# Sixteen more up tiles in the wide form: its range begins at tile 48 where it began at tile 64

## The chip, the cores and the metric

The kernel runs on one NeuronCore of one Trainium2 chip. The metric is the time of one execution on the device in microseconds, measured on that core. The time of before is 1027.47 us, the median of three runs (1025.19, 1027.47, 1031.39).

## What is computed

One decoder layer for a prompt of 256 tokens and eight samples of four tokens: a joint projection, two attention mixers, an output projection with LayerNorm, and then the part in which the change lies, PEER. There each token's query picks, from 128 x 128 experts per head, 16 experts for each of 8 heads. The reference computes it as

```
a = gelu(einsum('cpkd,cd->cpk', u_tab[e], h))
out = einsum('cpk,cpkd->cd', g * a, v_tab[e])
```

with `u_tab` and `v_tab` of 16,384 rows by 1,024. For the 256 prompt tokens the kernel takes every expert instead of gathering: it multiplies h by the whole of u, 128 tiles of 128 experts ("up"), applies GELU, weighs the result by a gate that is zero where an expert was not picked, and multiplies by the whole of v, 128 tiles again ("down"). The 32 sample tokens gather their rows of u and v instead.

## The kernel before, in words

The numbers need nearly fp32 accuracy, so each product is made of three: operands are split into a high part rounded to the fast fp32 form and a low part (the rest), and hi*hi, hi*lo and lo*hi are added in PSUM.

**One up tile.** SP loads a tile of u (128 x 1024 floats, 512 KB) into one of four ring slots. ScalarE writes its high part `w_hi` with a copy (`high`, line 1198, the copy at 1204), VectorE its low part `w_lo` by a subtraction (`low`, line 1579, the instruction at 1583), TensorE multiplies eight blocks of 128 rows with h. `halves` gives the semaphore values at which the low part of a tile is there. The result of tile n lies in PSUM bank n % 4, first 256 columns. ScalarE applies GELU (line 1456) into `u_out`, which has two buffers, and SP stores it to DRAM (`store`, line 460; `activations`), from where the down tiles read it back. 32 results, those of positions 64 to 95, stay in SBUF (`keep`) and are not stored; tiles are numbered here by position in the order of work. Because ring slots, PSUM banks and `w_hi` are all four deep, the high part of tile n + 4 is made after tile n's product is done.

**Two forms of the product.** The narrow form (`project` with `parts`, lines 639 and 630) has for each block three products of 256 columns: w_hi with h_hi (L635), w_hi with h_lo (L636), w_lo with h_hi (L637). The wide form (`project_wide`, line 1085) has two: w_hi with h_lo and h_hi side by side, 512 columns in one product (L1091), and w_lo with h_hi, 256 columns (L1093), into the bank's second half. The two halves of the bank then have to be added: ScalarE copies the second half to SBUF (`u_half`, line 1451), VectorE adds it to the first (line 1595), and only then comes the GELU. There is one buffer `u_half`.

**Which tile has which form** is said by `WIDE` (line 54), a range of positions. TensorE runs narrow loops over tiles 4 to `WIDE.start`, a wide loop over the range, and narrow ones again (lines 1097 to 1102). VectorE's program is laid out by Python: `low_next` (line 1588) puts out the next low part, ahead of it the addition for the tile four earlier if that one is in `WIDE`, and behind it a row dot (`row_dot`, line 1606) of the samples if one is due. The candidate lists and the routing of the prompt tokens (`top16`, `route`) are interleaved with `low_next` by `pace`, which counts work and not time. So VectorE runs everything in one fixed order. ScalarE has `gelu` (line 1441) and `gelu_then_high` (line 1458): narrow tiles have GELU, then the cast of tile n + 4; wide ones have the wait for the store, the copy to `u_half`, the cast, the wait for the addition and the GELU. Before, `gelu` takes its form from the first tile of its loop.

**Order on the queues.** SP alternates (`experts_in`, line 464): for each r it waits till the low part of the tile four earlier is there, issues the load of tile n, then waits for the GELU of tile n - 6 and issues its store. Before tile n's result is touched, ScalarE waits till the store of tile n - 2 has landed (line 1449). GpSimd meanwhile issues small indirect DMAs (`gates_out`, line 570) and gathers of 512 KB (`row_of_u`, line 578), each gather behind a row dot. At the first kept tile ScalarE waits once for the ninth row dot (line 1484), because `keep` lies over the candidate lists.

Of the kernel before, what the change touches and what calls it, by code (L numbers as in the profile page):

```python
# [26 lines left out]
KEPT, KEPT_AT = 32, 64  # L27
# [23 lines left out]
NCAND = sum(ROWLEN)  # L51
PACE, PACE_Q, PACE_LISTS, PACE_ROUTE = 1.2, 2.0, 2 / 3, 0.5
LIST_DOTS = 8
WIDE = range(64, 104)
SLOPES = [2.0 ** (-(h + 1)) for h in range(8)]


# [77 lines left out]
def trunk(nc, xT, w_in, w_gate, w_out, w_q, keysT, uT, v, u_rows, w1, pe_cmp, w2, vecs, ln2_rows, cache_sb, cache_nsa,  # L135
# [3 lines left out]
    with ctx:  # L139
# [259 lines left out]
        def filled(n):  # L399

            return n % 4, 16 * (n // 4 + 1)
# [3 lines left out]
        U_ALONE = NE - GN // 8  # L405
# [6 lines left out]
        def place(n):  # L412

            if AT_OUT <= n < AT_Q:
                return OUT_PLACE[n - AT_OUT]
            return n % 4 if n < AT_U + U_ALONE else 4 + n % 2
# [206 lines left out]
        def _(pe):  # L623
# [28 lines left out]
            def halves(i, n):  # L652

                return part_lo[n % 4], 2 * i + (2 * (n // 4) + 1), 2 * i + (2 * (n // 4) + 2)
# [424 lines left out]
            def experts_up(first, last):  # L1079
                with pe.Fori(first, last) as i:  # L1080
                    for r in range(4):
                        pe.wait_ge(u_act, 4 * i + r + 1)
                        project((AT_U + r) % 4, h_parts, r, halves(i, AT_U + r), width=DT)

            def project_wide(slot, bank, lows):

                for kd in range(KD):
                    if kd % 4 == 0:
                        pe.wait_ge(lows[0], lows[1 + kd // 4])
                    block_ = slice(kd * 128, (kd + 1) * 128)  # L1090
                    mm(ps[:, bank, :].rearrange("p (a t) -> p a t", a=2), w_hi[slot][:, block_],  # L1091
                       h_both[:, :, kd * T:kd * T + DT], start=kd == 0, stop=False)
                    ins = mm(ps[:, bank, DT:2 * DT], w_lo[slot][:, block_], h_hi[:, kd, 0:DT], start=False, stop=kd == KD - 1)  # L1093
                    if kd % 4 == 3:
                        ins.then_inc(w_mm, 1)

            experts_up(1, WIDE.start // 4)
            with pe.Fori(WIDE.start // 4, WIDE.stop // 4) as i:
                for r in range(4):
                    pe.wait_ge(u_act, 4 * i + r + 1)  # L1100
                    project_wide((AT_U + r) % 4, r, halves(i, AT_U + r))
            experts_up(WIDE.stop // 4, U_ALONE // 4 - 1)

# [84 lines left out]
        def _(act):  # L1188
# [9 lines left out]
            def high(ring_slot, arrived, slot, half=None, used=None):  # L1198

                act.wait_ge(full[ring_slot], arrived)  # L1200
                if used is not None:
                    act.wait_ge(w_mm, used)
                x = slice(0, D) if half is None else slice(half * D // 2, (half + 1) * D // 2)
                nc.scalar.copy(w_hi[slot][:, x], ring[:, ring_slot, x]).then_inc(part_hi, 2 if half is None else 1)  # L1204
# [233 lines left out]
            act.sem_inc(u_act, 4)  # L1438
            act.sem_inc(g_sb, 4)

            def gelu(i, r, first=0):

                act.wait_ge(w_mm, 8 * i + 2 * (AT_U + first + r + 1))
                if first == KEPT_AT:
                    out = keep[:, bass.ds(4 * i + r, 1), :].rearrange("p a t -> p (a t)")
                else:
                    out, kept_before = u_out[:, r % 2, :], KEPT if first > KEPT_AT else 0
                    if first + r >= 2:
                        act.wait_ge(spill[r % 2], 32 * i + 16 * ((first + r - kept_before) // 2))
                if first >= WIDE.start and first < WIDE.stop:  # L1450
                    nc.scalar.copy(u_half[:, :], ps[:, r, DT:2 * DT]).then_inc(u_lo, 1)
                    n = AT_U + first + r + 4
                    slot, value = filled(n)
                    high(slot, 16 * i + value, place(n))
                    act.wait_ge(u_sum, 4 * i + (first - WIDE.start + r + 1))
                A(out, ps[:, r, 0:DT], ACT.Gelu_apprx_tanh).then_inc(u_act, 1)  # L1456

            def gelu_then_high(i, r, first=0):

                gelu(i, r, first)  # L1460
                n = AT_U + first + r + 4
                slot, value = filled(n)
                high(slot, 16 * i + value, place(n))
# [14 lines left out]
            A(pick[:, 0, 2, 64:128], pick[:, 0, 2, 64:128], ACT.Exp).then_inc(rt_exp, 1)  # L1478
            for r in range(4):
                gelu_then_high(3, r, 4)  # L1480
            with act.Fori(4, KEPT_AT // 4 - 1) as i:
                for r in range(4):
                    gelu_then_high(i, r, 4)
            act.wait_ge(u_dot, LIST_DOTS + 1)
            assert WIDE.start == KEPT_AT and WIDE.stop == U_ALONE - 8
            with act.Fori(0, KEPT // 4) as i:
                for r in range(4):
                    gelu(i, r, KEPT_AT)
            with act.Fori(0, (U_ALONE - 8 - KEPT_AT - KEPT) // 4) as i:
                for r in range(4):  # L1490
                    gelu(i, r, KEPT_AT + KEPT)

            act.wait_ge(rt_exp_in, 4)
            A(sgate[:, :], sgate[:, :], ACT.Exp).then_inc(rt_exp, 1)
# [862 lines left out]
```

## Time and profile before

| | |
|---|---|
| median of three runs | 1027.47 us (1025.19 to 1031.39) |
| the profiled execution: its time | 1030.56 us |
| the profiled execution: span from first to last instruction | 1028.8 us |
| TensorE busy | 1011.6 us, 98% |
| VectorE busy | 818.3 us, 80% |
| ScalarE busy | 546.0 us, 53% |
| GpSimd busy | 371.5 us, 36% |
| mean granted TensorE clock | 0.995 |

Durations below come from the one profiled execution, whose own time lies 3.1 us over the median. In the rows PE is TensorE, PEld its weight loads, DVE VectorE, ACT ScalarE, POOL GpSimd and SP SyncE; L1583 is line 1583 of the kernel. Matmuls overlap one another, so a product's spacing to the next, not its own duration, is what it costs. A row that ends in brackets names how long the engine was idle just ahead of the instruction and what ended that.

### The profile page before, as it was taken

The numbers are of one execution on the slowest core, as the hardware profiler recorded it, in microseconds if no ns is written. First come the engines' busy times: TensorE is split into PE (matmuls) and PEld (weight loads), VectorE is DVE, ScalarE is ACT, GpSimd is POOL, SyncE is SP. The second block draws the span as 40 slices with busy tenths as digits, with TensorE's granted clock in tenths as the row PEclk, the third lists the DMA queues.
The fourth block names the chain that finished last, engine by engine and source line by source line (L and its number), as shares of the span: only waits on it lengthen the run. The fifth ranks groups of instructions, "written<-read, shape, count | busy, mean of one in ns | idle before, by whom it ended". The sixth has DMA issues, their size and how long they took to land.

```text
span 1028.8 us, 21635 instructions
## 1 busy us (share of the span) xinstructions
PE 1011.6 (98%) x6669; PEld 898.4 (87%) x6669; DVE 818.3 (80%) x1819; ACT 546.0 (53%) x1036; POOL 371.5 (36%) x287
## 2 busy tenths in 40 slices
PE   8999999999999999999999999999999999999997
PEld 7997747999999999998888999988878888888876
DVE  5344277786889988879998699988878888999888
ACT  5435576454545444456555655555555555555553
POOL 0244400000067888888887875011110101111000
PEclk9999999999999999999999999999999999999999
DMA  8756889344588899999999966778888889888763
GB/s 273 258 219 219 304 271 314 122 154 134 189 216 229 216 295 292 332 325 283 279 279 273 259 130 178 254 238 310 323 298 307 282 296 308 305 301 308 254 223 126
DMA packets 123281, 261.77 MB, mean 254 GB/s; under 512 B 29104, under 2 KB 70080, under 8 KB 121408
## 3 DMA queue, kind: packets, MB, share of 16 engines
q1 hardware_dynamic: 89280, 198.31, 57.3%
q0 software_dynamic: 33664, 62.30, 22.1%
q10 hardware_dynamic: 288, 0.59, 0.2%
q8 instruction: 21, 0.34, 0.1%
q14 instruction: 28, 0.23, 0.1%
HBM read 236.83 MB, written 26.38 MB: 256 GB/s over the span
## 4 chain that ended last, share of the span: by engine, by line
PE 59%; DMA 2%; DVE 1%; issue 1%; DVEq 0%; ACT 0%; SPq 0%; ACTq 0%
PE ps L1147 10%; PE ps L1149 10%; PE ps L1148 10%; PE ps L1091 7%; PE ps L636 5%; PE ps L635 5%; PE ps L637 5%; PE ps L1093 4%; PE ps L1124 3%; DMA a_in<-activations 1%; DMA ring<-in_v_dram 1%; DVE w_lo L1583 1%; PE ps L1138 0%; PE ps L1169 0%; DVE y_lo L2124 0%
## 5 line engine op out<-in xcount | busy, mean ns | idle before, releaser
L1583 DVE TENSOR_TENSOR w_lo<-ring,w_hi 128x512 fp32r<-128x512 f32 (+1 forms) x440 | 383.7, 879 | 109.2 <-ACT w_hi L1204 91.8
L1204 ACT CAST w_hi<-ring 128x512 fp32r<-128x512 f32 (+1 forms) x437 | 338.0, 774 | 79.1 <-PE ps L1149 54.1
L574 POOL DMA_INDIRECT gates<-spread_out,spread_at x128 | 241.7, 1888 | 131.4 <-DVE spread_out L2039 82.4
L635 PE MATMUL ps<-h_both,w_hi 128*128 128x256 f32 (+1 forms) x808 | 234.4, 290 | 2.0 <-DVE w_lo L1583 1.8
L636 PE MATMUL ps<-h_both,w_hi 128*128 128x256 f32 (+1 forms) x808 | 230.1, 285 | 0.0
L637 PE MATMUL ps<-h_both,w_lo 128*128 128x256 f32 (+1 forms) x808 | 228.9, 283 | 0.0
L1147 PE MATMUL ps<-w_hi,y_hi 128*128 128x512 f32 x496 | 193.4, 390 | 1.5 <-DVE y_lo L2124 1.3
L1148 PE MATMUL ps<-w_hi,y_lo 128*128 128x512 f32 x496 | 193.0, 389 | 0.0
L1149 PE MATMUL ps<-w_lo,y_hi 128*128 128x512 f32 x496 | 193.0, 389 | 0.0
L635 PEld LDWEIGHTS ps<-h_both,w_hi 128*128 128x128 f32 x808 | 153.6, 190 | 3.5 <-DVE w_lo L1583 2.2
L636 PEld LDWEIGHTS ps<-h_both,w_hi 128*128 128x128 f32 x808 | 153.2, 190 | 0.0
L637 PEld LDWEIGHTS ps<-h_both,w_lo 128*128 128x128 f32 x808 | 151.8, 188 | 0.0
L600 POOL DMA_INDIRECT vrow<-in_v_dram,expert x32 | 36.4, 1136 | 256.2 <-DVE sacc L2149 235.4
L1147 PEld LDWEIGHTS ps<-w_hi,y_hi 128*128 128x128 f32 x496 | 93.1, 188 | 22.3 <-DVE y_lo L2124 2.6
L1091 PE MATMUL ps<-h_both,w_hi 128*128 128x512 f32 x320 | 111.5, 392 | 0.0
L1149 PEld LDWEIGHTS ps<-w_lo,y_hi 128*128 128x128 f32 x496 | 93.1, 188 | 19.6
L1148 PEld LDWEIGHTS ps<-w_hi,y_lo 128*128 128x128 f32 x496 | 93.1, 188 | 19.2
L1456 ACT ACTIVATE u_out<-ps 128x256 f32<-128x256 f32 x96 | 37.0, 385 | 125.7 <-PE ps L637 77.9
L1093 PE MATMUL ps<-h_both,w_lo 128*128 128x256 f32 x320 | 89.9, 281 | 0.0
L1527 ACT CAST y_hi<-a_in 128x256 fp32r<-128x256 f32 x92 | 37.5, 408 | 66.5 <-PE ps L1149 66.3
L1091 PEld LDWEIGHTS ps<-h_both,w_hi 128*128 128x128 f32 x320 | 60.0, 188 | 13.4
L1093 PEld LDWEIGHTS ps<-h_both,w_lo 128*128 128x128 f32 x320 | 60.4, 189 | 0.0
(392 smaller groups left out, 1493.8 us busy)
## 6 DMA issues: line engine op xcount, KB each, us to landing
ring<-in_uT_dram SPq DMA_DIRECT2D x128, 512.0 KB, 4.3
ring<-in_v_dram SPq DMA_DIRECT2D x128, 512.0 KB, 4.3
activations<-u_out SPq DMA_DIRECT2D x96, 128.0 KB
a_in<-activations SPq DMA_DIRECT2D x96, 128.0 KB, 4.2
ring<-in_w_in_dram SPq DMA_DIRECT2D x21, 512.0 KB, 5.5
gates<-spread_out SPq DMA_DIRECT2D x8, 1024.0 KB, 9.1
ring<-in_w_q_dram SPq DMA_DIRECT2D x16, 512.0 KB, 3.9
gates<-gates POOLq DMA_DIRECT2D x8, 1024.0 KB, 7.6
```

What stands on the lines that cost most here:

```text
L574: nc.gpsimd.indirect_dma_start(g_dram, bass.IndirectOffsetOnAxis(ap=spread_at[:, m:m + 1], axis=0), spread_out[:, m:m + 1], None, compute_ ...
L635: mm(out, hi, hi_, start=start, stop=False)
L636: mm(out, hi, lo_, start=False, stop=False)
L637: return mm(out, lo, hi_, start=False, stop=stop)
L1091: mm(ps[:, bank, :].rearrange("p (a t) -> p a t", a=2), w_hi[slot][:, block_], h_both[:, :, kd * T:kd * T + DT], start=kd == 0, stop=False)
L1093: ins = mm(ps[:, bank, DT:2 * DT], w_lo[slot][:, block_], h_hi[:, kd, 0:DT], start=False, stop=kd == KD - 1)
L1147: mm(out, hi, w_hi[slot][:, x], start=False, stop=False, skip_group_check=True)
L1148: mm(out, lo, w_hi[slot][:, x], start=False, stop=False, skip_group_check=True)
L1149: return mm(out, hi, w_lo[slot][:, x], start=False, stop=stop, skip_group_check=True)
L1204: nc.scalar.copy(w_hi[slot][:, x], ring[:, ring_slot, x]).then_inc(part_hi, 2 if half is None else 1)
L1527: nc.scalar.copy(y_hi[:, r % 2, :], a).then_inc(y_h, 1)
L1583: V.tensor_tensor(w_lo[slot][:, x], ring[:, ring_slot, x], w_hi[slot][:, x].bitcast(F32), ALU.subtract).then_inc(part_lo[ring_slot], 2 if ...
```

## The change

The range of wide tiles begins at 48. ScalarE's loop over tiles 20 to 63 is cut in two, the second of them wide, and `gelu` is told its form by an argument. TensorE's loops and VectorE's additions follow from `WIDE`. Nothing else changes: loads, stores, the kept tiles, the lists and the dots stay in their order.

```diff
@@ -51,7 +51,7 @@
-WIDE = range(64, 104)
+WIDE = range(48, 104)
@@ -1438,7 +1438,7 @@
-            def gelu(i, r, first=0):
+            def gelu(i, r, first=0, wide=False):
 
                 act.wait_ge(w_mm, 8 * i + 2 * (AT_U + first + r + 1))
                 if first == KEPT_AT:
@@ -1447,7 +1447,7 @@
                     out, kept_before = u_out[:, r % 2, :], KEPT if first > KEPT_AT else 0
                     if first + r >= 2:
                         act.wait_ge(spill[r % 2], 32 * i + 16 * ((first + r - kept_before) // 2))
-                if first >= WIDE.start and first < WIDE.stop:
+                if wide:
                     nc.scalar.copy(u_half[:, :], ps[:, r, DT:2 * DT]).then_inc(u_lo, 1)
                     n = AT_U + first + r + 4
                     slot, value = filled(n)
@@ -1478,17 +1478,20 @@
-            with act.Fori(4, KEPT_AT // 4 - 1) as i:
+            with act.Fori(4, WIDE.start // 4 - 1) as i:
                 for r in range(4):
                     gelu_then_high(i, r, 4)
+            with act.Fori(WIDE.start // 4 - 1, KEPT_AT // 4 - 1) as i:
+                for r in range(4):
+                    gelu(i, r, 4, True)
             act.wait_ge(u_dot, LIST_DOTS + 1)
-            assert WIDE.start == KEPT_AT and WIDE.stop == U_ALONE - 8
+            assert WIDE.start <= KEPT_AT and WIDE.stop == U_ALONE - 8
             with act.Fori(0, KEPT // 4) as i:
                 for r in range(4):
-                    gelu(i, r, KEPT_AT)
+                    gelu(i, r, KEPT_AT, True)
             with act.Fori(0, (U_ALONE - 8 - KEPT_AT - KEPT) // 4) as i:
                 for r in range(4):
-                    gelu(i, r, KEPT_AT + KEPT)
+                    gelu(i, r, KEPT_AT + KEPT, True)
```

## Rows read from the trace of the kernel before

**Rows 1.** The page, busy shares and the 40 slices.
```profile
PE 1011.6 (98%) x6669; PEld 898.4 (87%) x6669; DVE 818.3 (80%) x1819; ACT 546.0 (53%) x1036; POOL 371.5 (36%) x287
...
PEclk9999999999999999999999999999999999999999
```

**Rows 2.** TensorE's own waits from 372 us on: total us, times, longest us.
```profile
PE ps L635 <- DVE w_lo L1583: 1.4, 1, 1.4
PE ps L1147 <- DVE y_lo L2124: 1.3, 1, 1.3
```

**Rows 3.** First products of a block, narrow (372 to 457.4 us) and wide: min/median/max ns.
```profile
L635 PE MATMUL ps<-h_both,w_hi x240: 277/282/385, 371.8 to 457.1; 128*128 128x256 f32 x120
...
L1091 PE MATMUL ps<-h_both,w_hi x320: 389/393/394, 457.5 to 568.6; 128*128 128x512 f32 x160
```

**Rows 4.** A stretch: us, busy PE, PEld, DVE, ACT, POOL, clock, DMA, GB/s.
```profile
411.70:457.50 45.80, 45.80 (x387) 45.80 (x386) 37.43 (x104) 21.23 (x33) 38.19 (x24) 1.00 1.02 320
```

**Rows 5.** ScalarE's GELUs, 411.7 to 459 us, and their longest wait.
```profile
L1456 ACT ACTIVATE u_out<-ps x17: 384/385/389, 412.9 to 458.6; 128x256 f32<-128x256 f32 x17
...
  DMA activations<-u_out: 20.4, 13
```

**Rows 6.** Groups by line and shape, whole span: busy us, mean ns, idle before.
```profile
L1595 DVE TENSOR_TENSOR ps<-ps,u_half 128x256 f32<-128x256 f32 x40 | 17.1, 428 | 2.2 <-ACT u_half L1451 1.9
...
L1451 ACT COPY u_half<-ps 128x256 f32<-128x256 f32 x40 | 14.9, 373 | 13.8 <-PE ps L1093 8.8 <-DMA activations<-u_out 4.9
```

**Rows 7.** VectorE's groups, 411.7 to 457.5 us, the first.
```profile
L1583 DVE TENSOR_TENSOR w_lo<-ring,w_hi 128x1024 fp32r<-128x1024 f32 x18 | 21.7, 1224 | 8.4 <-ACT w_hi L1204 8.0
```

**Rows 8.** Timeline of ScalarE, wide tiles with a store: start us, us, instruction.
```profile
549.74 0.37 ACT L1451 COPY u_half<-ps 128x256 f32<-128x256 f32 x1
...
553.00 0.38 ACT L1456 ACTIVATE u_out<-ps 128x256 f32<-128x256 f32 x1
...
557.68 0.37 ACT L1451 COPY u_half<-ps 128x256 f32<-128x256 f32 x1 [1.60 <-DMA activations<-u_out]
...
558.90 0.39 ACT L1456 ACTIVATE u_out<-ps 128x256 f32<-128x256 f32 x1
...
570.36 0.37 ACT L1451 COPY u_half<-ps 128x256 f32<-128x256 f32 x1 [1.31 <-DMA activations<-u_out]
```

**Rows 9.** Timeline of VectorE: the ninth row dot; the low part of tile 63.
```profile
423.25 1.23 DVE L1609 CUSTOM_DVE_ANT_0 urow<-urow,hrow 128x1024 f32<-128x1024 f32 x1
...
450.67 1.23 DVE L1583 TENSOR_TENSOR w_lo<-ring,w_hi 128x1024 fp32r<-128x1024 f32 x1 [0.45 <-ACT w_hi L1204]
```

**Rows 10.** Timeline of ScalarE at tile 64.
```profile
460.49 0.38 ACT L1451 COPY u_half<-ps 128x256 f32<-128x256 f32 x1 [0.58 <-PE ps L1093]
460.75 1.06 ACT L1204 CAST w_hi<-ring 128x1024 fp32r<-128x1024 f32 x1
```

**Rows 11.** Timeline of SP: four stores of u_out.
```profile
406.90 0.35 SPq L462 DMA_DIRECT2D activations<-u_out  x1
...
453.04 0.34 SPq L462 DMA_DIRECT2D activations<-u_out  x1
...
553.40 0.34 SPq L462 DMA_DIRECT2D activations<-u_out  x1
...
567.28 0.35 SPq L462 DMA_DIRECT2D activations<-u_out  x1
```

**Rows 12.** DMA in 411.7 to 457.5 us, then in 546 to 572 us: median us to landing.
```profile
ring<-in_uT_dram SPq DMA_DIRECT2D x17, 512.0 KB, 6.2
...
DMA packets 3841, 7.06 MB, mean 271 GB/s; under 512 B 1462, under 2 KB 2339, under 8 KB 3841
...
ring<-in_uT_dram SPq DMA_DIRECT2D x9, 512.0 KB, 4.8
```

**Rows 13.** Timeline of ScalarE: the first and last of the 13 waited GELUs.
```profile
412.90 0.39 ACT L1456 ACTIVATE u_out<-ps 128x256 f32<-128x256 f32 x1 [1.11 <-DMA activations<-u_out]
...
458.58 0.39 ACT L1456 ACTIVATE u_out<-ps 128x256 f32<-128x256 f32 x1 [2.13 <-DMA activations<-u_out]
```

## The prediction, made before the changed kernel ran

> **What bounds the kernel now.** I read the page's busy shares and slices first: TensorE is busy for 98% of the span and its granted clock is full in every slice [rows 1]; the list of TensorE's own waits then has, after 372 us, just two of 1.4 and 1.3 us [rows 2]. So TensorE's instruction stream sets the time, and everything else counts only when it makes TensorE wait. The change touches sixteen up tiles, 48 to 63. By the forms of their products they lie ahead of the first wide product at 457.5 us [rows 3]. A narrow tile is 24 products (8 blocks by 3). The 240 first products between 371.8 and 457.1 us give 85.3 / 239 = 0.357 us a block, 2.855 us a tile; the 320 wide ones between 457.5 and 568.6 us give 111.1 / 319 = 0.348 us a block, 2.786 us a tile [rows 3]. Tile 48 then starts at 457.5 - 16 x 2.855 = 411.8 us. From there to 457.5 us VectorE works 37.4 of 45.8 us, and the DMA engines are full: share 1.02, 320 GB/s [rows 4]. The last thing to see there is that ScalarE, ahead of its GELUs, waits 20.4 us in 13 of 17 cases for an earlier store of u_out to land [rows 5]. That wait costs nothing today, because the ring runs four tiles ahead; it is what the change leans on.
>
> **The change, part by part.** *TensorE.* Each of the sixteen tiles loses 8 products of 256 columns with their weight loads, and 8 others grow from 256 to 512 columns. By the tile times above it saves 2.855 - 2.786 = 0.069 us a tile, **1.1 us** in all, the only gain. The sum of columns is unchanged, so there is no second source. The wide block's 0.348 us stands on 320 of them [rows 3]. TensorE: Matmul & The Clock Gate in the Trainium skill, section Back-to-back issue gap, gives about 131 ns for a 512-column product in a sustained stream, and N/2.4 + 2.5 ns for an isolated one; by the first a wide tile could not last over 2.1 us and the change would give some 12 us, by the second it would give 0.3 us. The rows contradict the first and lie near the second.
>
> *VectorE.* Sixteen additions of 428 ns [rows 6] are 6.8 us more. Its low parts of this stretch come with 8.4 us of idle time, 8.0 of it behind ScalarE's casts [rows 7]; 45.8 - 37.4 = 8.4 again. It fits, with 1.5 us left (the stretch itself shrinks by 1.1), so I cost it at nothing on the path; without that cover it costs up to 6.8 us less the room worked out below. The row dots and candidate lists stay where they are in VectorE's program; behind each addition wait that tile's GELU and the low part of the tile four later.
>
> *ScalarE.* Sixteen copies of 373 ns [rows 6] are 6.0 us. It is busy 21.2 of 45.8 us [rows 4], so the copies themselves are covered. What matters is the order. In the narrow form the GELU comes first, then the cast; in the wide form copy, cast, wait for the addition, GELU. In a tile that finds everything ready the copy starts at 557.68 and the GELU at 558.90, 1.22 us later [rows 8]; where VectorE or the ring is late it is more: the first of the eight wide tiles with a store has 549.74 and 553.00, 3.26 us [rows 8]; over these eight the delay averages 1.8 us. For tiles 48 to 63, with lists on VectorE, I take 1.8 too (bounds 1.2 and 3.3). ScalarE's one-time wait for the ninth row dot at tile 64 is covered: that dot starts at 423.25 us [rows 9], and tile 64 comes to ScalarE at 460.49 us [rows 10].
>
> *SP and the stores.* u_out has two buffers, so work on tile n's result may begin when the store of n - 2 has landed. The store is issued 0.4 us behind its GELU where SP is free (553.00 [rows 8], 553.40 [rows 11]); I take 0.5, since a load's issue often lies between. In the narrow form a round for two tiles is 0.5 plus the landing; in the wide form it is 1.8 + 0.5 plus the landing, against the 5.57 us that TensorE takes for two wide tiles. So a landing up to 5.2 us is free now, and only up to 3.3 us afterwards. SP also issues the loads of the ring in the same queue, one between two stores, so a late GELU holds back the next load as well; loads land in 6.2 us (median) in this stretch and 4.8 us in 546 to 572 us [rows 12]. Their chain (GELU, store and load issue 1.1, landing 6.2, cast and GELU 1.2) is 8.5 us for three tiles, 2.8 a tile, as long as TensorE's and no longer.
>
> What the landing will be is the unknown. **Upper bound:** in the 13 waited cases of rows 5 it ran from store to GELU at first 6.0 us (406.90 to 412.90), at last 5.5 (453.04 to 458.58) [rows 11, 13], and 5.2 in the mean. **Lower bound:** in the five waited cases of the wide tiles with a store it was at first 4.3 (553.40 to 557.68), at last 3.1 (567.28 to 570.36) [rows 8, 11], and 3.55 in the mean, with the DMA engines at 271 GB/s [rows 12]. These eight tiles went without a stall of TensorE [rows 2]. I take 4.2 us, between them and nearer to the second: a chain that has become slower also asks for fewer transfers, which shortens the queue it waits in. The Trainium skill points the same way (DMA: Bandwidth & Descriptors, Latency and other measured facts: HBM access 0.2 us on average and 2 us at high load); the two stretches agree in sign, and no run so far shows the 0.2 us.
>
> *Room.* TensorE needs the low part of tile n + 4 three tiles after it ends tile n, 8.36 us. From the copy it takes 0.27 to the cast, 1.06 for the cast, 0.1 and 1.22 for the low part [rows 9, 10], 2.7 us. So ScalarE may fall 5.6 us behind while VectorE is free; in the busiest place today only 2.7 is left (low part of tile 63 from 450.67 to 451.90, its tile from 454.65) [rows 9].
>
> *Sum.* Landing 4.2: 6.5 us for two tiles, 3.25 a tile, 0.46 over TensorE's; sixteen tiles fall 7.4 us behind, 5.6 are room, TensorE stalls 1.8 us. Behind tile 63 there are no stores for 32 tiles and the delay drains. 1.8 - 1.1 = **+0.7 us**. The profiled execution took 1030.56 us (span 1028.8), 3.1 us over the median of the three runs, so 1031.3 for it and 1028.2 for the median.
>
> **Rivals.** *The room holds everything.* With the landing at 3.55 a round is 5.85 us, sixteen tiles fall 2.2 us behind and TensorE never waits: -1.1 us, 1026.4. For it speak the eight wide tiles with stores; against it that they had fewer row gathers beside them and no lists.
>
> *The stores' round trip becomes the bound.* With the landing at 5.2 a round is 7.5 us, 3.75 a tile, and sixteen tiles fall 15.4 us behind; less 5.6 of room and 1.1 of gain that is +8.7 us, with the smallest room of 2.7 it is +11.6: 1036 to 1039. It is slower than before from a landing of 4.1 us, and by over 0.5% (5.1 us, about what a measurement of this kernel can tell from no change) from 4.8 us. For it: 5.2 us is what these very tiles show, and DMA is full in them. Against: stores and loads come more slowly once it binds.
>
> *VectorE takes over.* If its waits of 8.0 us behind the casts stay as they are, the additions make it 6.8 us late; with room 2.7 to 5.6 TensorE stalls 1.2 to 4.1 us, net 0 to +3: 1027.5 to 1030.5. This lies in the forecast's own range.
>
> *The wide product costs less here than among the kept tiles.* To bring 5.1 us, a wide tile would have to fall to 2.855 - 5.1 / 16 = 2.54 us, 0.317 a block, where the quickest and slowest of its products differ by 5 ns in all 320 [rows 3]: 0.01, and about 1022 us. (The 131 ns of the page named above would be such a case.)
>
> *The change does not do what it says.* The form is chosen in three places: TensorE's loop, the test on VectorE and ScalarE's flag. All three follow, so this has 0.02; the time would be 1027.5.
>
> **How the numbers follow.** Forecast (stalls of 0.5 to 5 us, VectorE's case in it) 0.53; room holds 0.22; round trip 0.20; no effect 0.02; cheaper wide product 0.01; something unseen 0.02, taken as faster. Slower by over 0.5% is the round trip's 0.20 and 0.02 from the forecast's tail: 0.22. Faster by over 0.5% is 0.03, as 1.1 us is the whole gain. Within 0.5% is the rest, 0.75. The three runs of before spread from 1025.19 to 1031.39, so the lower end is -1.1 and 2.3 for that spread, 1024; the upper end takes in the middle of the round trip's case, 1036.
>
> **What would show it.** Right: the first product of the wide form comes near 411.8 us; tiles of 2.79 us up to about the tenth; ScalarE's waits for stores well over 20 us and now ahead of the copies; one or a few stalls of TensorE behind low parts, 1 to 5 us in all, between 435 and 475 us; landings near 4.2 us. Wrong: no stall at all (room holds), stalls over 6 us with landings of 5 and more (round trip), or VectorE without idle time there while the copies wait for nothing (VectorE's case). A gain over 5 us, or stalls far behind 500 us, would mean a mechanism that I have not seen.

## The result and the profile after

| | before | after |
|---|---|---|
| median (range) of 20 runs each, us | 1027.7 (1024.94 to 1031.97) | 1033.48 (1028.65 to 1040.73) |
| ratio | | 1.0048, interval 1.0033 to 1.0063 |
| profiled execution, us (span) | 1030.56 (1028.8) | 1030.98 (1029.3) |

The change makes the kernel 4.9 us slower (1027.7 x 0.0048; 3.4 to 6.5 by the interval). The two profiled executions differ by 0.4 us only, and that must not be read as the effect. The one of before lay about 3 us above its median and the one of after 2.5 us below: before had a wait of TensorE at 372 us [rows 2], another at 364 us, and a low clock about 160 us, all ahead of tile 48 and absent there in after. So I compare a stretch: the tiles 48 to 103, by their first products. The forms table of after gives its wide ones; the second line is the narrow form.

```profile
L1091 PE MATMUL ps<-h_both,w_hi x448: 388/393/632, 406.3 to 569.8; 128*128 128x512 f32 x150
L635 PE MATMUL ps<-h_both,w_hi x568: 277/282/384, 270.4 to 666.7; 128*128 128x256 f32 x190
```

There are 448 wide products for 320: 56 tiles. They take 569.8 - 406.3 = 163.5 us. Before, the same tiles took 568.6 - 411.8 = 156.8 us [rows 3]. The median of a product is as before; the maximum of 632 ns is new. The busy shares and the chain that ended last, from the page, and TensorE's waits from 400 to 575 us:

```profile
PE 1011.0 (98%) x6541; PEld 890.6 (87%) x6541; DVE 824.6 (80%) x1835; ACT 549.5 (53%) x1052; POOL 362.0 (35%) x287
```
```profile
PE 84%; DVE 8%; DMA 3%; ACT 2%; issue 2%; ACTq 0%; DVEq 0%; SPq 0%
PE ps L1147 11%; PE ps L635 11%; PE ps L1149 11%; PE ps L1148 11%; PE ps L636 11%; PE ps L637 11%; PE ps L1091 4%; PE ps L1124 3%; DVE w_lo L1586 3%; PE ps L1093 2%; DMA activations<-u_out 2%; PE ps L723 2%; ACT w_hi L1204 1%; DVE urow L1612 1%; PE ps L1018 1%
```
```profile
PE ps L1091 <- DVE w_lo L1586: 4.8, 5, 2.1
```

TensorE is still 98% busy, so the first line tells nothing. The chain does: stores of u_out have 2% of it and low parts 3%; in the chain of before, which could be followed back over only 63% of the span, u_out does not stand. And TensorE now waits for low parts ahead of wide products. Measured from block to block, the lost time is 2.29 us (at 447.61), 1.69 (462.11), 0.38 (465.38), 0.73 (477.32), 0.20 (527.75) and 0.48 (545.02): 5.8 us. The view of waits has less because it counts only from the end of the product ahead. The block behind each of these six is 0.07 to 0.11 us longer than the others, 0.5 us in all. 5.8 and 0.5 less the gain of 1.1 is +5.2 us, near the runs' +4.9, but it is one execution.

The largest of them can be followed back through four engines. POOL, SP, ScalarE, VectorE, TensorE in the timeline of after (start, duration, instruction, and in brackets the idle time ahead with its releaser):

```profile
437.09 0.99 POOL L581 DMA_INDIRECT urow<-in_u_rows_dram,expert  x1 [3.75 <-DVE sact L1612]
```
```profile
437.77 0.35 SPq L462 DMA_DIRECT2D activations<-u_out  x1
438.31 0.34 SPq L468 DMA_DIRECT2D ring<-in_uT_dram  x1
439.47 0.35 SPq L462 DMA_DIRECT2D activations<-u_out  x1
440.04 0.50 SPq L431 DMA_DIRECT2D ring<-in_uT_dram  x1
```
```profile
444.91 0.37 ACT L1451 COPY u_half<-ps 128x256 f32<-128x256 f32 x1 [5.61 <-DMA activations<-u_out]
445.18 1.05 ACT L1204 CAST w_hi<-ring 128x1024 fp32r<-128x1024 f32 x1
```
```profile
445.31 0.43 DVE L1598 TENSOR_TENSOR ps<-ps,u_half 128x256 f32<-128x256 f32 x1 [3.78 <-ACT u_half L1451]
446.33 1.23 DVE L1586 TENSOR_TENSOR w_lo<-ring,w_hi 128x1024 fp32r<-128x1024 f32 x1 [0.58 <-ACT w_hi L1204]
```
```profile
447.61 0.50 PE L1091 MATMUL ps<-h_both,w_hi 128*128 128x512 f32 x1 [2.13 <-DVE w_lo L1586]
```

One gather, two stores and two loads are issued within 3 us. The store of 437.77 lands at 444.91, 7.1 us later, and ScalarE stands for 5.6 of them **ahead of its copy**. Behind the copy stand the cast, VectorE's addition (VectorE is empty for 3.78 us) and the low part, and TensorE starts 2.7 us after the copy does, the distance that the prediction gave to this chain. Before, the same kind of wait stood ahead of GELUs [rows 5]. The next cast stood behind it there too; what is new is that copy, cast and addition stand between the wait and the next store.

The sum of ScalarE's waits for the stores did not grow, it moved ahead of the copies: from 400 to 575 us before had 25.1 us ahead of GELUs and 4.9 ahead of copies. ScalarE in after:

```profile
ACT u_half L1451 <- DMA activations<-u_out: 20.1, 13, 5.6
ACT u_out L1456 <- DMA activations<-u_out: 3.2, 2, 2.8
ACT w_hi L1204 <- DMA ring<-in_uT_dram: 2.1, 2, 1.5
ACT u_half L1451 <- PE ps L1093: 6.4, 4, 2.6
```

The last line names TensorE's products, and that can't be. The four waits end at 416.23, 420.40, 426.06 and 433.03 us, ahead of the copies of tiles 50, 51, 53 and 55. TensorE had no stall before 447.61, so by its 2.786 us a tile from 406.3 the products of these tiles were done 1.6 to 4.4 us earlier. The code has the copy wait for nothing else but the store of tile n - 2. So these 6.4 us are waits for stores as well: 26.5 us ahead of copies and 3.2 ahead of GELUs, 29.7 in all, for 30.0 before.

Beside it the clock fell once. The windows of after (us, TensorE, weight loads, VectorE, ScalarE, POOL, granted clock, DMA share, GB/s):

```profile
445.00:448.00 3.00, 0.87 (x6) 0.51 (x5) 2.10 (x8) 2.81 (x5) 1.54 (x2) 1.00 0.44 57
450.00:451.00 1.00, 1.00 (x4) 0.81 (x4) 1.00 (x2) 0.36 (x3) 0.00 (x0) 0.50 0.98 400
453.00:456.00 3.00, 3.00 (x19) 2.66 (x18) 2.80 (x4) 1.17 (x2) 2.39 (x3) 1.00 0.77 218
```

TensorE was busy for 0.87 of three microseconds, and from 449 to 452.6 us it had the half clock: 5.5 blocks at 0.64 us for 0.348, about 1.6 us. That makes up the profile's +6.7 (5.8 + 0.5 + 1.6 - 1.1 = 6.8). The two are not independent: while TensorE is slow, ScalarE catches up, so by the reckoning of the room below the stall at 462.11 would have been longer without the low clock. Over the runs the clock is no part of the +4.9: reckoned over every run as time x (1 - mean granted clock), the clock costs 3.3 us in before and 3.6 in after, within the uncertainty of 0.5.

### The profile page after: what moved, and what is told of

It is laid out like the page before. It is cut to its first block, busy times and chain, and to the rows that moved or that the text cites. A ratio compares the mean times of both kernels' runs of the same rounds, so it can differ in the third digit from the quotient of the medians.

```text
span 1029.3 us, 21433 instructions
## 1 busy us (share of the span) xinstructions
PE 1011.0 (98%) x6541; PEld 890.6 (87%) x6541; DVE 824.6 (80%) x1835; ACT 549.5 (53%) x1052; POOL 362.0 (35%) x287
## 4 chain that ended last, share of the span: by engine, by line
PE 84%; DVE 8%; DMA 3%; ACT 2%; issue 2%; ACTq 0%; DVEq 0%; SPq 0%
PE ps L1147 11%; PE ps L635 11%; PE ps L1149 11%; PE ps L1148 11%; PE ps L636 11%; PE ps L637 11%; PE ps L1091 4%; PE ps L1124 3%; DVE w_lo L1586 3%; PE ps L1093 2%; DMA activations<-u_out 2%; PE ps L723 2%; ACT w_hi L1204 1%; DVE urow L1612 1%; PE ps L1018 1%
## 5 line engine op out<-in xcount | busy, mean ns | idle before, releaser
L574 POOL DMA_INDIRECT gates<-spread_out,spread_at x128 | 234.9, 1835 | 130.4 <-DVE spread_out L2042 82.5
L635 PE MATMUL ps<-h_both,w_hi 128*128 128x256 f32 (+1 forms) x680 | 198.4, 292 | 0.3 <-issue 0.3
L636 PE MATMUL ps<-h_both,w_hi 128*128 128x256 f32 (+1 forms) x680 | 193.8, 285 | 0.0
L637 PE MATMUL ps<-h_both,w_lo 128*128 128x256 f32 (+1 forms) x680 | 192.8, 284 | 0.0
L1091 PE MATMUL ps<-h_both,w_hi 128*128 128x512 f32 x448 | 158.3, 396 | 4.8 <-DVE w_lo L1586 4.8
L635 PEld LDWEIGHTS ps<-h_both,w_hi 128*128 128x128 f32 x680 | 129.2, 190 | 1.3 <-issue 1.3
L636 PEld LDWEIGHTS ps<-h_both,w_hi 128*128 128x128 f32 x680 | 128.9, 190 | 0.0
L1093 PE MATMUL ps<-h_both,w_lo 128*128 128x256 f32 x448 | 126.5, 282 | 0.0
L1091 PEld LDWEIGHTS ps<-h_both,w_hi 128*128 128x128 f32 x448 | 84.8, 189 | 25.4 <-DVE w_lo L1586 4.3
```

The lines of the kernel that those rows point to most:

```text
L574: nc.gpsimd.indirect_dma_start(g_dram, bass.IndirectOffsetOnAxis(ap=spread_at[:, m:m + 1], axis=0), spread_out[:, m:m + 1], None, compute_ ...
L635: mm(out, hi, hi_, start=start, stop=False)
L636: mm(out, hi, lo_, start=False, stop=False)
L637: return mm(out, lo, hi_, start=False, stop=stop)
```

## The experiments

Every stretch and stall below comes from one profiled execution of its kernel, the ratios from 10 to 12 runs (5 of start_32). Three theories. **Stores:** the copy, cast and addition now stand behind the store of tile n - 2, and its landing is sometimes 7 us. **VectorE:** sixteen more additions on an engine that has 1.5 us left make the low parts late by themselves. **Loads:** a later GELU holds back SP's next load of the ring. Edits are against the kernel after unless said. "Tiles 48 to 103" is the first to the last first-product; 447 blocks by 2.786 / 8 are 155.7 us.

**late_wait.** The wait for the store moves behind the copy, cast and addition.

```
-                    if first + r >= 2:
-                        act.wait_ge(spill[r % 2], 32 * i + 16 * ((first + r - kept_before) // 2))
+                stored = lambda: first != KEPT_AT and first + r >= 2 and act.wait_ge(
+                    spill[r % 2], 32 * i + 16 * ((first + r - kept_before) // 2))
+                if not wide:
+                    stored()
                 if wide:
...
                     act.wait_ge(u_sum, 4 * i + (first - WIDE.start + r + 1))
+                    stored()
                 A(out, ps[:, r, 0:DT], ACT.Gelu_apprx_tanh).then_inc(u_act, 1)
```

> The change, but in wide tiles ScalarE waits for the store of u_out only ahead of the GELU, which is what writes u_out; the copy to u_half and the cast of tile n + 4 no longer wait for it. Store theory (the round trip of the stores delays copy, cast and low part until TensorE starves): the stalls of 48 to 75 go from 5.4 us to under 1 us, the slow clock behind the first of them goes too, and the time is 0 to 1.5 us below before (ratio 0.9985 to 1.000). VectorE theory (sixteen additions overload VectorE, stores are only its messenger): the additions are all there, so at least half of the 4.9 us loss stays (ratio 1.0025 or more). Load theory (a late GELU holds back SP's next load): GELUs are still as late, so loss stays and ScalarE's waits for ring loads grow.

Ratio to before 1.0019 (0.9996 to 1.0042). Its forms table, and ScalarE's waits from 345 to 575 us:

```profile
L1091 PE MATMUL ps<-h_both,w_hi x448: 389/393/394, 415.2 to 570.9; 128*128 128x512 f32 x150
```
```profile
ACT u_out L1459 <- DMA activations<-u_out: 22.3, 12, 4.9
ACT w_hi L1204 <- DMA ring<-in_uT_dram: 10.2, 14, 1.9
```

155.7 us, no stall in 48 to 103, the maximum of a product back at 394 ns. All 56 additions are there, and ScalarE still waits up to 4.9 us for stores. Only what stands behind that wait has changed. The waits for loads grew from 2.1 us in after to 10.2 and no stall came of them, against the loads theory. The ratio leaves the kernel 2 us above before, and its interval holds both what the stores theory (up to 1.000) and what VectorE's theory (1.0025 or more) expected: here only the trace decides.

**four_bufs_after** and **four_bufs_before.** Four u_out buffers up to tile 63: the wait is for the store of n - 4. The second is the same edit of the kernel before, against which the first is to be held.

```
-                sp.dma_start(dst, u_out[:, r % 2, :]).then_inc(spill[r % 2], 16)
+                sp.dma_start(dst, u_four[(r - 6) % bufs]).then_inc(spill[(r - 6) % 4], 16)
...
-                    if first + r >= 2:
-                        act.wait_ge(spill[r % 2], 32 * i + 16 * ((first + r - kept_before) // 2))
+                    if first < KEPT_AT:
+                        out = u_four[r]
+                        if first + r >= 4:
+                            act.wait_ge(spill[r], 16 * i + 16 * (r // 2 + first // 4))
...
```

> The change with four u_out buffers for tiles 0 to 63 (a wait is for the store of tile n - 4, not n - 2); the order on ScalarE is as in the change. Store theory: the wait for a store, 20.1 us in 13 tiles of the change, falls under 2 us, TensorE's stalls in 48 to 75 under 1 us, the time 0 to 1.5 us below before. VectorE theory: ratio to before 1.0025 or more. Load theory: loss stays at least in half, since SP's order is as in the change.

> The kernel before with four u_out buffers for tiles 0 to 63: the control for the run above. All theories: the waits for stores go (20.4 us in 411.7 to 459), TensorE did not wait there, so the time moves by less than 1.5 us either way (ratio 0.9985 to 1.0015). The two or three short stalls of the narrow tiles near 360 to 372 us could go and give up to 2 us.

1.0000 (0.9974 to 1.0025) and 1.0007 (0.9991 to 1.0024). The change with four buffers, forms and ScalarE's waits from 345 to 575 us:

```profile
L1093 PE MATMUL ps<-h_both,w_hi x448: 389/393/394, 409.7 to 565.4; 128*128 128x512 f32 x150
```
```profile
ACT w_hi L1206 <- DMA ring<-in_uT_dram: 12.2, 10, 2.5
ACT u_half L1459 <- DMA activations<-u_out: 1.2, 2, 0.7
```

Again 155.7 us and no stall. The waits for stores are nearly gone (1.2 us), and ScalarE waits for loads of the ring instead, which costs TensorE nothing. The loss of 4.9 us is gone too. Beside its own baseline the change is now 0.7 us faster by the ratios (1.0000 / 1.0007); 1.1 was to be had, and the intervals hold 0 and 1.1 alike. Of the runs that take out the stalls of tiles 48 to 67 with all sixteen additions in place, this one, gelu_first and small_gathers have intervals that lie wholly below the 1.0033 where the change's begins; late_wait's, up to 1.0042, does not.

**start_56.** The wide form from tile 56.

```
-WIDE = range(48, 104)
+WIDE = range(56, 104)
```

> The wide range begins at 56: half the dose. Store theory: 0.55 us gained; eight tiles fall behind by what exceeds a round of 5.57 us, which is mostly room, so a loss clearly under half of 4.9 us, 0 to 2 us (ratio 1.000 to 1.002), except where two stores of 7 us fall into the eight tiles. VectorE theory: half the additions, half the loss, about 2.5 us (1.0024).

1.0013 (0.9994 to 1.0033). Its 384 wide products take 134.1 us for 133.4, one stall of 0.49 at 542 us. Eight tiles stay within the room, as 8 x 0.62 = 5.0 us of delay (3.41 a tile, measured in after, for 2.79) are about the room, and sixteen don't. The ratio itself separates nothing: +1.3 us with an interval from -0.6 to +3.4 holds the 0 to 2 of the stores theory and the 2.5 of VectorE's.

**gelu_first.** In tiles 48 to 63 the GELU goes ahead of copy and cast, as in the narrow form. It then takes the first half of the bank before the addition, so these sixteen results lack the second half; the work on every engine is the same.

```
+                if wide and first < KEPT_AT:
+                    A(out, ps[:, r, 0:DT], ACT.Gelu_apprx_tanh).then_inc(u_act, 1)
                 if wide:
...
                     act.wait_ge(u_sum, 4 * i + (first - WIDE.start + r + 1))
+                    if first < KEPT_AT:
+                        return
```

> The change with all its instructions, but in tiles 48 to 63 ScalarE runs the GELU before the copy and the cast, as the narrow form does; these sixteen GELUs leave out the second half of the product, and all work on every engine remains. Store theory: a round is again 0.5 us plus the landing, so TensorE's stalls in tiles 48 to 75 fall from 5.4 us to under 1 us, the 56 wide tiles take 155.7 us as with a late wait or four buffers (163.5 in the change), ratio to before 0.998 to 1.001. VectorE theory: nothing is taken from VectorE, so stalls and loss stay, ratio 1.003 or more.

1.0004 (0.9983 to 1.0024). Wide forms of TensorE and its waits for them from 345 to 575 us:

```profile
L1091 PE MATMUL ps<-h_both,w_hi x448: 388/393/470, 412.8 to 570.3; 128*128 128x512 f32 x150
```
```profile
PE ps L1091 <- DVE w_lo L1590: 0.9, 2, 0.6
```

The store is issued early again, and from 48 to 67 only 0.10 us is lost (at 465.83). What remains are 0.72, 0.19 and 0.48 us at 478, 528 and 545 us: the same three as in after. I come back to them below.

**cast_first.** The kernel before, with only the order changed: in narrow tiles 48 to 63 the cast goes ahead of the GELU, which delays GELU and store by one cast, 1.05 us.

```
+                if cast_first:
+                    n = AT_U + first + r + 4
+                    slot, value = filled(n)
+                    high(slot, 16 * i + value, place(n))
...
```

> The kernel before, tiles 48 to 63 narrow as there, but ScalarE runs the cast of tile n + 4 ahead of the GELU in these sixteen: no addition, no copy, no wide product, just a GELU and a store about 1.0 us later. Store theory: the round for two tiles goes from 0.5 to 1.5 us plus the landing; with landings of 5.2 us that is 6.7 us against 5.71, sixteen tiles fall 8 us behind, room 5.6 and TensorE stalls 0 to 3 us: tiles 48 to 103 take 157 to 160 us (157.1 before), ratio 1.000 to 1.003. VectorE theory: nothing changes, 157.1 us and no stall in tiles 48 to 75.

0.9997 (0.9976 to 1.0018), no stall from 373 to 575 us. Tiles 48 to 103 take 156.8 us as before, where 157 to 160 was expected. One microsecond of delay behind the store's wait does not bind. The change has 1.7. The expectation had put in landings of 5.2 us, and they were shorter: the 13 waited ones of tiles 48 to 63 run from 3.2 to 5.5 us, mean 4.35, so a round is about 0.5 + 1.0 + 4.3 = 5.8 us for TensorE's 5.71.

**start_32** and **four_bufs_32.** The wide form from tile 32, with two and with four buffers.

```
-WIDE = range(48, 104)
+WIDE = range(32, 104)
```

> The wide range begins at 32: thirty-two tiles with a store instead of sixteen. Store theory: 2.2 us gained, the round trip binds for twice as long and the room is used once, so stalls more than double: 10 to 16 us of them, loss 8 to 14 us (ratio 1.008 to 1.014). If the loss came from one unlucky pair of slow stores rather than from a round that binds, it would be less than double, ratio under 1.006.

> Four u_out buffers and a wide range that begins at 32. Store theory: no wait for a store binds, gain of 32 x 0.069 = 2.2 us against before and 1.1 against four buffers with a start at 48: ratio 0.997 to 0.999. VectorE theory: in tiles 32 to 48 the first candidate lists stand beside the additions (VectorE 2.5 us of lists for two tiles), so stalls of TensorE come back there, 1 to 5 us, ratio 1.000 to 1.004.

1.0137 (1.0106 to 1.0168), +14 us, and 1.0038 (1.0018 to 1.0059), +3.9 us. Forms and TensorE's waits from 345 to 575 us in start_32, and the forms in four_bufs_32:

```profile
L1091 PE MATMUL ps<-h_both,w_hi x576: 388/393/771, 362.8 to 577.8; 128*128 128x512 f32 x192
```
```profile
PE ps L1091 <- DVE w_lo L1586: 8.7, 10, 2.3
```
```profile
L1093 PE MATMUL ps<-h_both,w_hi x576: 388/393/629, 364.4 to 572.1; 128*128 128x512 f32 x192
```

Stall-free they would take 575 x 0.3483 = 200.3 us; they take 215.0 and 207.7. Twice the tiles in the new form cost nearly three times as much, as a room that is spent once would have it. Four buffers bring back half of the lost time in the two traces and 10 of the 14 us in the runs (start_32's profiled execution was the quickest of its five). Stalls of 2.66 us at 373 (before has one of 1.4 at 372 [rows 2]) and 1.06 at 435 us remain, and VectorE is busy 51.2 of the 55 us from 410 to 465. I had expected more from them, and this is the first sign that VectorE's theory is wrong for the sixteen tiles, not in general.

**four_bufs_double_add.** Four buffers and, in 48 to 63, a second addition of 128x256 whose result nobody reads, to measure VectorE's margin.

```
+                    if made < KEPT_AT:
+                        link(V.tensor_tensor(y_low_idle, con[:, 0:DT], con[:, 0:DT], ALU.add))
```

> Four u_out buffers, wide from 48, and in tiles 48 to 63 VectorE makes a second, unused addition of the same size behind each real one (6.8 us more, and a short wait each). VectorE has some 4.5 of 45 us free there in the run with four buffers, so this overfills it by 3 to 4 us; with the room of up to 5.6 us TensorE stalls 0 to 2 us in tiles 48 to 103 (155.7 us without). If VectorE had been the cause in the change, doubling its dose must bring back at least the change's 4 us of stalls even without store waits.

1.0014 (0.9997 to 1.0030). Forms and TensorE's waits from 345 to 575 us:

```profile
L1094 PE MATMUL ps<-h_both,w_hi x448: 388/393/501, 410.4 to 573.2; 128*128 128x512 f32 x150
```
```profile
PE ps L1094 <- DVE w_lo L1596: 4.4, 6, 1.3
```

A miss: 162.8 us, 7.1 over the stall-free 155.7, where stalls of 0 to 2 us were expected. In this execution sixteen additions more (6.8 us) appear nearly whole. But it was the slowest of the ten runs, 1035.2 us where the median is 1030.3, and the ratio is only 1.4 us over that of four_bufs_after, with intervals that overlap. So the trace shows that the change's own sixteen fit and the next don't; what the next cost in a usual run stays open.

**small_gathers.** POOL's gathers of rows from the ninth on bring 128 columns in place of 1024, so the sample tokens' results are other ones; the row dots keep their size.

```
+                cols = D if k < 8 else 128
+                nc.gpsimd.indirect_dma_start(urow[:, k % 4, 0:cols], None, u_rows.rearrange("n (a c) -> (n a) c", c=cols),
+                                             at_slot(k)).then_inc(ug_in[k % 4], 16)
```

> The change, but from the ninth on each gather of a u row for the sample tokens takes 128 columns and not 1024 (64 KB for 512; the values gathered are other ones, the row dots are of full size). This takes some 4 MB of 14.7 out of the DMA queues in tiles 48 to 63. Store theory with the queue as its cause: waited landings of stores fall from a mean over 5 us to under 4, none of 7, TensorE's stalls in 48 to 75 from 4.4 us to under 1, 56 wide tiles in 155.7 to 157 us, ratio 0.997 to 1.001. If landings are long for another reason (the load that is issued just ahead of the store), they stay over 5 us and so do the stalls.

0.9992 (0.9973 to 1.0011). Forms and ScalarE's waits ahead of the copy:

```profile
L1093 PE MATMUL ps<-h_both,w_hi x448: 389/393/394, 414.2 to 569.8; 128*128 128x512 f32 x150
```
```profile
ACT u_half L1453 <- DMA activations<-u_out: 12.6, 11, 1.8
```

155.7 us by the block starts (414.15 to 569.85), no stall, with two buffers and the wait where the change puts it. The longest wait for a store ahead of a copy is 1.8 us for 5.6, and the waited landings of tiles 48 to 63 are 1.8 to 4.1 us, mean 3.0. So the long landings appear only with the full gathers.

**four_bufs_later_dots** and **four_bufs_later_dots_64.** Four buffers, and the first eight row dots two steps (tiles) later in VectorE's list; wide from 48 and from 64.

```
-                return 3 * j if j < LIST_DOTS else 3 * LIST_DOTS + 2.1 * (j - LIST_DOTS)
+                return 3 * j + 2 if j < LIST_DOTS else 3 * LIST_DOTS + 2.1 * (j - LIST_DOTS)
```

> Four u_out buffers, wide from 48, and the first eight row dots two low parts later in VectorE's program, so that VectorE does not wait for the first gathers (2.4 and 1.3 us at 362 and 367 us before, behind which TensorE stalls 1.9 us and sometimes gets its lower clock). Expected: no stall between 345 and 575 us; 1.1 us from the wide form and 2 to 3 us from the dots against before: ratio 0.996 to 0.998.

> The same with the wide range from 64, as before: the control that gives the worth of the wide form alone once nothing waits. Expected 1.1 us slower than the run with 48: ratio 0.997 to 0.999.

1.0002 (0.9984 to 1.0020) and 0.9975 (0.9959 to 0.9990). The second is the quickest kernel of the study, 2.6 us under before, and the only one whose interval lies wholly below 1. It has the wide form **where it was before**. The forms of both, first from 48, then from 64:

```profile
L1093 PE MATMUL ps<-h_both,w_hi x448: 389/393/394, 409.5 to 565.2; 128*128 128x512 f32 x150
```
```profile
L1093 PE MATMUL ps<-h_both,w_hi x320: 389/393/394, 454.9 to 566.0; 128*128 128x512 f32 x160
```

Neither has a stall of TensorE from 345 to 575 us. With a narrow tile at 2.855 us, tile 48 of the second starts at 454.9 - 45.7 = 409.2, and its last wide product is at 566.0: 156.8 us, against 155.7 in the first. So the gain of 1.1 us is in the profiled execution, but the runs show none, and both expectations missed. Part of it is the clock: time x (1 - mean granted clock) is 4.5 us in the mean of the first's runs and 3.1 in the second's. Without it both take 1023.3 us (standard errors 0.6 and 0.3), which neither shows a gain of 1.1 nor rules it out. That stays open. So does which half of the edit brings the 2.6 us: the four buffers alone gave 1.0007.

## Why the prediction was right and where it was wrong

Forecast 1028.2, or +0.7 us; measured +4.9, in the range of 1024 to 1036. That it lies within 0.5% is luck: 0.48%, with an interval from 0.33 to 0.63. The case that came is the forecast's mechanism with three times its stalls (5.8 us for 1.8), half way to the round-trip rival's +8.7. The wide range, made for that rival, is what held it.

*The bound* is right: TensorE's stream sets the time. But its clock was not full in every slice of before, as I read from [rows 1]: the digit 9 stands for 90% or more, and falls at 8 and 161 us are hidden in it.

*The gain* is right: 155.7 us without stalls against 156.8, by the forms of late_wait and of before.

*VectorE's additions covered* is right for these sixteen (four_bufs_after: all additions, no stall), and that little more is left fits double_add. The rival "VectorE takes over" falls as the cause in 48 to 63.

*The delay of the GELU* was put at 1.8 us behind the copy and measures 1.73 in the mean over the sixteen.

*The landing* is the term that was mis-sized. I took 4.2 us, between 3.55 and 5.2, on the ground that a slower chain asks for fewer transfers. The eight waits that the view gives to stores in tiles 48 to 63 are landings of 4.34, 3.47, 4.54, 7.14, 7.23, 4.12, 6.74 and 7.34 us, mean 5.6. The four that it gives to TensorE add 2.31, 4.92, 1.97 and 5.19: the mean of the twelve is 4.9. Where a copy did not wait, its start bounds the landing (6.4, 5.9, 2.8 and 2.5 us), so all sixteen have a mean of at most 4.8. The ground was right as far as it went: DMA moved 275 GB/s in this stretch for 320 before, and cast_first, also slower by a microsecond, had 4.35 us for 5.2. What it left out are four landings of about 7 us. They come in two pairs. The first store of each (437.77, 452.67) has a gather 0.7 and 0.5 us ahead and a second store and two loads within 2.3 us behind it. At the stores of 430.99 and 446.54 a gather is as near ahead but the next store is over 3 us behind: 4.54 and 4.12 us. At 413.92 the second store is there, but the gather comes 0.2 us behind the first: 2.31 us. small_gathers shows that the gathers are needed; that the pairing is too is read from one trace and not tested. The kernel before had long ones as well, 7.7 us at the most (429.72 to 437.39), and my mean of 5.2 hid them. The HBM access latency of 2 us at high load, from the Trainium skill, DMA: Bandwidth & Descriptors, Latency and other measured facts, is below all of these landings but one; it could give a direction and no size.

*The round* came out at 3.41 us a tile (tile 48's copy at 409.88, tile 64's at 464.44) for 3.25, so about 10 us behind for 7.4. By my own formula that is a landing of 2 x 3.41 - 1.73 - 0.5 = 4.6 us. But the tiles did not fall behind evenly. Against TensorE's unstalled pace the copy is 3.5 us late at tile 57, 7.9 at tile 58 and 11.3 at tile 62; the two steps are landings of 7.14 and 6.74 us. The *room* of 5.6 us is right: 7.9 less the stall of 2.29 ahead of tile 62 is 5.6, and 11.3 less the 5.7 us that TensorE had lost when tile 66 began is 5.6 again. The first stall so came at tile 62, the fifteenth, and not at about the tenth. The stalls up to tile 67 are 4.36 us for 1.8.

*"Behind tile 63 the delay drains"* is the second step that failed. Late work does not drain where VectorE is full. Two windows of after:

```profile
406.30:466.50 60.20, 56.32 (x313) 48.75 (x312) 47.16 (x140) 28.72 (x52) 41.13 (x26) 0.97 0.89 275
466.50:546.00 79.50, 78.58 (x449) 68.46 (x448) 74.13 (x97) 44.33 (x87) 66.37 (x37) 1.00 0.89 277
```

VectorE works 47.2 of 60.2 us in the first and 74.1 of 79.5 in the second, which has the candidate lists. Behind a low part that came late stands an instruction of 2.3 us:

```profile
473.30 2.29 DVE L2016 TENSOR_TENSOR step<-posf,con 128x2048 bf16<-128x2048 f32 x1
475.62 0.43 DVE L1598 TENSOR_TENSOR ps<-ps,u_half 128x256 f32<-128x256 f32 x1
475.96 1.22 DVE L1586 TENSOR_TENSOR w_lo<-ring,w_hi 128x1024 fp32r<-128x1024 f32 x1
```
```profile
477.32 0.47 PE L1091 MATMUL ps<-h_both,w_hi 128*128 128x512 f32 x1 [0.57 <-DVE w_lo L1586]
```

That is 1.41 us of stalls in tiles that the change does not touch. They stand where ScalarE comes late out of tile 63. From TensorE's start of tile 64 to ScalarE's copy of it pass 9.6 us in after, 8.6 in start_32, 8.0 in four_bufs_double_add, 6.9 in gelu_first, 6.5 in four_bufs_32 and 6.4 in start_56, and all six have the stall of 0.48 us near 545 us. It is 5.4 in late_wait, 4.1 in four_bufs_after, 3.9 in small_gathers and 3.0 in before, and none of these has it. So the stalls are not a matter of VectorE's additions alone, which late_wait and small_gathers have too. In gelu_first ScalarE was late because of stores as well: its GELU of tile 63 waited 3.8 us for one, with copy and cast behind it. The two errors, 4.36 - 1.8 and 1.41, make 4.0 of the 4.2 us between forecast and result.

*What the text said would be seen:* stalls between 435 and 475 us, 1 to 5 in all (4.36, right); ScalarE's waits ahead of the copies (right), "well over 20 us" (26.5, right, though not over what they were); landings near 4.2 (half right: 4.9 over the twelve, with four of about 7); the first wide product near 411.8 (406.3, as the waits and the low clock ahead of it were absent); no stalls far behind 500 us (wrong, 0.20 and 0.48 us at 528 and 545).

## What to carry to other kernels

Where a change puts work between the wait for a buffer and the store that frees the next one, add up the whole round (that work, the issue, the landing) and hold it against the time that the other engine takes for as many tiles as there are buffers. Take the landing from the stretch itself with its worst cases, as the mean hides them. A wait that costs nothing today says nothing of what it will cost. Put the wait next to the one instruction that needs it, or add a buffer. Where a view names a releaser that had long been done, look in the code for what else the instruction waits for. And before saying that a delay drains, look at the busy share of every engine in the stretch behind.

## What the runs showed of the hardware

In the stretch of after, the twelve waited stores of 128 KB landed in 2.0 to 5.2 us or, four of them, in 6.7 to 7.3 us. Before, the waited ones of the same tiles ran from 3.0 to 7.7 us with no gap between, so the two groups are this execution's. With the gathers cut to an eighth they were 1.8 to 4.1 us. The first of each long pair had a gather 0.5 to 0.7 us ahead and a second store and two loads within 2.3 us.

From 345 to 580 us the granted clock fell to half after six idles of TensorE: of 2.13 us in after, 2.33 and 2.13 in start_32, 2.50 in four_bufs_32, 2.06 in small_gathers and 1.96 in late_wait. It began between the idle's end and 1.5 us later (at 449.1 us in after, for an idle that ended at 447.61; at 371 us in start_32, for one that ended at 371.00) and cost about 1.7 us each time. Idles of 1.60 us (start_56), 1.53 (after, at 462.11), 1.44 (gelu_first), 1.39 (cast_first) and 1.36 (before [rows 2]) had no fall behind them. But idles alone don't tell: all 14 profiled executions have one of 1.0 us near 141 us, and five of them have a fall within 2 us of it, six one at about 160 us with no idle just ahead, and three none. Reckoned from the granted clock, the clock costs 2.2 to 4.5 us in the mean of a kernel's runs, and part of the spread between runs goes with it.
